# Expert weights on separate semaphores, and down weights issued one expert later

## What is computed

```python
# 16 experts, the best 2 of one group of 4 for each token, width 256
def step(acc, xs):
    wg, wu, wd, cw = xs
    y = (jax.nn.silu(t @ wg) * (t @ wu)) @ wd
    return acc + y.astype(jnp.float32) * cw[:, None], None
acc, _ = lax.scan(step, jnp.zeros(t.shape, jnp.float32), (w_gate, w_up, w_down, comb.T))
```

## Time and profile before

| | us |
|---|---|
| median of 3 runs | 1970.52 |
| lowest and highest | 1969.63, 1974.61 |
| profiled execution, its own time | 1959.03 |
| its span, first to last instruction | 1957.4 |
| experts stage of layer 0, about | 1385 to 1545 |
| experts stage of layer 1, about | 1788 to 1957 |

### The profile page before, as it was taken

One profiled execution on the slowest core, in us unless ns is written; L12 is line 12 of the kernel. 1 busy time (PEld: TensorE's weight loads), 2 busy tenths in 40 slices (PEclk: granted clock), 3 DMA queues, 4 the chain that ended last, 5 costly groups with the idle time before them and its releaser, 6 DMA issues.

```text
span 1957.4 us, 25950 instructions
## 1 busy us (share of the span) xinstructions
PE 1897.8 (97%) x9760; PEld 1005.7 (51%) x9760; DVE 750.1 (38%) x1637; ACT 546.4 (28%) x1187; POOL 732.5 (37%) x1065
## 2 busy tenths in 40 slices
PE   8999999999999999999999999999998899999988
PEld 6644556656457455565665455654443344444433
DVE  1343443433221243434336563843532401334424
ACT  3243432214321334422124222742211221012110
POOL 0767676765666667676700012100110100001101
PEclk9999999999999999999999999999999999999999
DMA  7332343244344353333384312042799722047996
GB/s 292 123 109 101 127 148 121 87 144 142 137 169 141 105 199 107 135 138 116 138 335 162 129 38 86 2 181 98 284 366 369 252 91 86 30 186 256 362 377 247
DMA packets 71706, 328.70 MB, mean 168 GB/s; under 512 B 8680, under 2 KB 11174, under 8 KB 56998
## 3 DMA queue, kind: packets, MB, share of 16 engines
q1 hardware_dynamic: 41688, 217.00, 29.9%
q0 software_dynamic: 26736, 98.58, 14.5%
q10 hardware_dynamic: 3168, 11.54, 1.5%
HBM read 288.29 MB, written 38.80 MB: 167 GB/s over the span
## 4 chain that ended last, share of the span: by engine, by line
PE 88%; DMA 5%; DVE 3%; issue 2%; ACT 1%; DVEq 1%; SPq 0%; POOL 0%; ACTq 0%; POOLq 0%
PE psA L464 26%; PE psA L1815 10%; PE psA L456 9%; PE psA L1950 6%; PE psA L1852 6%; PE psA L627 6%; PE psSO L1968 4%; PE psT L443 3%; DMA pool_mem<-in_w_dn 3%; PE psA L505 3%; PE psSO L534 3%; PE psSO L544 2%; DVE pool_mem L2894 1%; PE psSO L565 1%; PE psSO L600 1%
## 5 line engine op out<-in xcount | busy, mean ns | idle before, releaser
L464 PE MATMUL psA<-gB,pool_mem 128*128 128x512 f32 x1024 | 455.3, 597 | 0.0
L395 POOL TENSOR_TENSOR pool_mem<-pool_mem,cs 128x256 f32<-128x256 f32 x448 | 269.3, 634 | 126.4 <-DMA pool_mem<-in_mod_w 125.8
L464 PEld LDWEIGHTS psA<-gB,pool_mem 128*128 128x128 f32 x1024 | 189.5, 190 | 224.2 <-issue 224.2
L399 POOL TENSOR_TENSOR pool_mem<-pool_mem 128x256 f32<-128x256 f32 x336 | 248.1, 766 | 30.9 <-issue 22.9
L1815 PE MATMUL psA<-pool_mem 128*128 128x512 f32 (+1 forms) x528 | 210.7, 558 | 6.0 <-DVE pool_mem L1584 3.4
L456 PE MATMUL psA<-pool_mem,gB 128*128 128x256 f32 (+2 forms) x768 | 190.8, 404 | 1.7 <-ACT gB L797 1.2
L1764 POOL DMA_INDIRECT pool_mem<-xs_scratch,idx x38 | 35.4, 932 | 391.0 <-DVE idx L2568 361.1
L456 PEld LDWEIGHTS psA<-pool_mem,gB 128*128 128x128 f32 x768 | 144.6, 191 | 44.3 <-issue 8.3
L1950 PE MATMUL psA<-pool_mem 128*32 128x512 f32 (+1 forms) x896 | 146.2, 618 | 10.9 <-DMA pool_mem<-in_w_dn 10.9
L1815 PEld LDWEIGHTS psA<-pool_mem 128*128 128x128 f32 x528 | 100.3, 192 | 109.8 <-issue 99.8
L1852 PE MATMUL psA<-pool_mem 128*128 128x512 f32 x256 | 113.9, 595 | 0.8 <-issue 0.8
(11 more groups left out here) (345 smaller groups left out, 2371.0 us busy)
## 6 DMA issues: line engine op xcount, KB each, us to landing
pool_mem<-in_w_gu SPq DMA_DIRECT2D x32, 2048.0 KB, 13.8
pool_mem<-in_mod_w POOLq DMA_DIRECT2D x56, 1024.0 KB, 7.8
pool_mem<-in_w_dn SPq DMA_DIRECT2D x32, 1024.0 KB, 12.6
pool_mem<-in_w_qk SPq DMA_DIRECT2D x24, 1024.0 KB, 5.1
ys_scratch<-pool_mem POOLq DMA_DIRECT2D x1, 11264.0 KB, 42.1
ys_scratch<-pool_mem ACTq DMA_DIRECT2D x22, 512.0 KB, 11.5
pool_mem<-in_odd_w_in SPq DMA_DIRECT2D x5, 2048.0 KB, 9.7
pool_mem<-in_w_out SPq DMA_DIRECT2D x4, 2048.0 KB, 8.1
```

The source lines that it names most:

```text
L395: nc.gpsimd.tensor_tensor(wm[:, b, k], wm[:, b, k], c_all[:, k].to_broadcast([P, MCH]), ALU.mult)
L399: nc.gpsimd.tensor_tensor(wm[:, b, k], wm[:, b, k], wm[:, b, n + k], ALU.add)
L464: m = nc.tensor.matmul(psA[:, n % 2, :], w(i), src[:, k, :], start=(i == 0), stop=(i == len(ks) - 1))
```

## The change

It gives gate and up weights the semaphores `gate_up_loaded` (five) and down weights `down_loaded` (three, by u modulo 3). The gate and up product waits for gate and up weights alone. The down product gets waits for its own down weights. Since there are three semaphores for up to five transfers, dn(u) is issued only when dn(u - 3) has landed. And in SyncE's list dn(u) moves behind gu(u + 1), for u = 4 to 14.

```diff
-LOADED = [32 * len(USES[b::EXP_BUFS]) for b in range(EXP_BUFS)]
+LOADED = [16 * len(USES[b::EXP_BUFS]) for b in range(EXP_BUFS)]
+DOWN_SEMS = 3
+DOWN_LOADED = [16 * len(USES[b::DOWN_SEMS]) for b in range(DOWN_SEMS)]
...
-                sp.dma_start(gu_w[b], rows(d["w_gu"][l][e])).then_inc(exp_loaded[b], 16)
+                sp.dma_start(gu_w[b], rows(d["w_gu"][l][e])).then_inc(gate_up_loaded[b], 16)
...
-                sp.dma_start(down_w[b], rows(d["w_dn"][l][e])).then_inc(exp_loaded[b], 16)
+                if l or u >= DOWN_SEMS:
+                    sp.wait_ge(down_loaded[u % DOWN_SEMS], DOWN_LOADED[u % DOWN_SEMS] * l + 16 * (u // DOWN_SEMS))
+                sp.dma_start(down_w[b], rows(d["w_dn"][l][e])).then_inc(down_loaded[u % DOWN_SEMS], 16)
...
+                behind = None
                 for u in range(EARLY + 1, EXPERTS):
                     e = expert_of(u)
                     load_gate_up(l, u, e)
-                    load_down(l, u, e)
+                    if behind:
+                        load_down(l, *behind)
+                    behind = (u, e)
+                load_down(l, *behind)
...
-                        pe.wait_ge(exp_loaded[u % EXP_BUFS], LOADED[u % EXP_BUFS] * l + 32 * (u // EXP_BUFS + 1))
+                        pe.wait_ge(gate_up_loaded[u % EXP_BUFS], LOADED[u % EXP_BUFS] * l + 16 * (u // EXP_BUFS + 1))
+
+                def down_weights(c):
+                    for r, _, _, _ in PARTS[c]:
+                        u = USES.index(r)
+                        pe.wait_ge(down_loaded[u % DOWN_SEMS], DOWN_LOADED[u % DOWN_SEMS] * l + 16 * (u // DOWN_SEMS + 1))
...
                 def down(c):
                     b = c % 2
+                    down_weights(c)
                     pe.wait_ge(ht_copied, RUNS * l + c + 1)
```

More of the change, by code:

```diff
@@ L1481, in per_layer @@
         return [sem(f"{name}{l}") for l in range(DEPTH)]
-    exp_loaded = [sem(f"exp_loaded{b}") for b in range(EXP_BUFS)]
+    gate_up_loaded = [sem(f"gate_up_loaded{b}") for b in range(EXP_BUFS)]
+    down_loaded = [sem(f"down_loaded{b}") for b in range(DOWN_SEMS)]
     idx_moved = sem("idx_moved")
@@ L1929, in gate_up_first @@
                         pe.wait_ge(gb_copied, (6, 8)[l])
-                        pe.wait_ge(exp_loaded[0], LOADED[0] * l + 32)
+                        pe.wait_ge(gate_up_loaded[0], LOADED[0] * l + 16)
                     for k in ks:
```

## The result

| | median of timed runs, us | range | profiled execution | span |
|---|---|---|---|---|
| before | 1970.52 (3 runs) | 1969.63 to 1974.61 | 1959.03 | 1957.4 |
| changed | 1943.35 (3 runs) | 1940.44 to 1943.80 | 1940.44 | 1938.9 |

The ratio is 0.9853, 95% interval 0.9827 to 0.9879: 27.2 us less between the medians, and 29.0 (23.8 to 34.1) by the ratio. The profiled executions differ by 18.6 us only, and the forecast was 20.5. The direction and the mechanism came out as forecast; the size, between the medians, was 6.7 us larger.

The account below looks back on a forecast made before the run. TensorE, busy nearly all the span, was taken to bound the kernel, so only its waits and slowed instructions could be won. 22.5 less 1.0 remaining and 1.0 added waits gave 20.5 us off the median: 1950.0 us, range 1943 to 1961.

Parts of the forecast that it names:

- The four waits and the slow clock behind them: TensorE's weight waits in both experts stages and the matmuls slowed after them: removing all saves at most 22.5 us.
- Run 9: Each layer's first weight wait, ahead of a gate and up product, 5.18 and 5.77 us: expected to vanish.
- Run 11, the count of bytes: Ahead of the last gate product: 41.0 MB in layer 0 at 370 GB/s, gu(15) landing at 1508.4 and 1913.6 us.
- Remaining waits: Weight waits left ahead of the last gate products: 1.0 us in all, bounds 0 and 1.9.
- Added waits on TensorE: 19 new waits per layer at the down products: 1.0 us in all, bounds nothing and 3.4 us.
- Added waits on SyncE: In SyncE's load queue, dn(u) waiting for dn(u - 3) to land: no cost.
- dn(14) and dn(15) at the end: Last down loads, now ending the load chain: landing at about 1514 us, 8 us before their down product needs them.
- The sum: Whole kernel: 22.5 - 1.0 - 1.0 = 20.5 us saved, subtracted from the median to give 1950.0 us.
- A: Rival, chance 0.20: rate stays 356 GB/s, waits of 3.2 and 4.4 us remain before the last gate products; 1958.3 us.
- B: Rival, chance 0.09: DMA engines bound the experts stages at 345 GB/s or less; gain only 5 us, 1965.5 us.
- C: Rival, chance 0.05: always-queued weight loads slow the gathers, so transposes wait in every run; slower, 1970 to 1990 us.
- D: Rival, chance 0.06: unprofiled runs hold longer weight waits, so more than 24 us is won; 1944 us.

Follow-up runs that it names:

- experiment 13: Kernel before, old order and semaphores, without five down-weight transfers (dn(8), dn(9), dn(10), dn(14), dn(15)) in both layers: median 1943.33 us, ratio 0.9896.
- experiment 3: Changed kernel with the loads back in the old order, so only the semaphores are split: median 1955.56 us, ratio 0.9931 to the kernel before.
- experiment 4: Kernel before with the new load order alone, one semaphore still covering both transfers of an expert: median 1962.63 us, ratio 0.9975.
- experiment 2: Changed kernel timed and traced again without any edit: median 1942.44 us, ratio 0.9873 to the kernel before.
- experiment 8: Changed kernel timed and traced a third time without any edit: median 1944.18 us, ratio 0.9883 to the kernel before.
- experiment 6: Changed kernel with every added wait at the down products written three times: median 1944.22 us, ratio 0.9885 to the kernel before.
- experiment 9: Kernel before with dn(4) issued behind gu(5) instead of ahead of it: median 1965.30 us, ratio 0.9995.
- experiment 10: Changed kernel with dn(4) put back directly behind gu(4): median 1942.14 us, ratio 0.9887 to the kernel before.

## Why the prediction was right in kind and short in size

**The four waits and the slow clock behind them (22.5 us).** Right. Against the 60.1 us of experiment 13, which has no such waits, the five traces of before give 22.1 to 24.0 us, mean 23.2; the profiled execution on which I summed gave 22.7. This term was short by 0.7.

**Run 9.** Right: no wait in either layer. Experiments 3 and 4 show that it takes both parts, the semaphore (own dn no longer counted) and the order.

**Run 11, the count of bytes.** Right in its result, by two errors that nearly cancel, which is luck. I took 370 GB/s for a queue that is never empty, and 380 was measured; I put 41.0 MB ahead of gu(15)'s landing, and 380 GB/s x 112.1 us = 42.6 MB came. It landed at 1507.7, 2.0 us ahead of a stage clock that itself ran 2.0 us early, so 1509.7 against my 1508.4. In layer 1 it landed at 1878.8 + 21.4 = 1900.2; that stage's first hidden transposes come 12.1 us earlier than before (1785.7), so 1912.3 against my 1913.6. Remaining waits: 0.3 us in this trace, 1.4 in experiment 2 and 1.6 in experiment 8, and by the table the changed kernel's stretches are 1.2 us above those with no waits, against 1.0 forecast.

**Added waits on TensorE (1.0 us).** Wrong in size. Experiment 6 puts them at nothing that can be measured, in timed runs and in a stretch of 92.7 us. My upper bound took the 0.09 us between two kinds of runs for the price of a wait.

**Added waits on SyncE, and dn(14) and dn(15) at the end.** Right: no matmul of a down product waited for weights (the weight loads ahead of them, which overlap other matmuls, show 3.0 us in five places), and gu(15) went out 21 us and dn(14) 9 us earlier than before. dn(14) and dn(15) had landed by 1513.2, against my 1514, and the down product of run 11 started at 1520.5.

**The sum.** The mechanism held; the step that failed is the size of the sum's terms. "Waits added on TensorE" was put at 1.0 us and measured nothing, and the ceiling, put at 22.5 from one execution, measured 23.2 as the mean of five. 23.2 less 1.2 of remaining waits is 22.0 us, where the sum had 22.5 - 1.0 - 1.0 = 20.5. That is 1.5 of the 6.7 us by which the result exceeded the forecast. The other 5.2 have no term in the sum, which was subtracted from a median 11.5 us above the execution that it was read from.

By the ratio, three sets of timed runs give 29.0 (23.8 to 34.1), 25.0 (21.0 to 29.1) and 23.0 us (18.5 to 27.3); by the medians 27.2, 23.8 and 21.6. The last two hold 22.0; the first, with three runs on each side, begins at 23.8. So part of the 5.2 is the draw of the first runs: before had a median of 1970.5 there and 1964.2 to 1966.3 in the four later sessions, while the changed kernel stayed at 1942.4 to 1944.2. The rest of it stays open. The traces put at most about 3.3 us outside the stretches, most of it around the start of layer 1's stage, where two of five traces of before lose 5.8 and 4.0 us and one of three of the changed kernel 2.4. Layer 0's start varies too: the profiled execution of before loses 2.7 us there. Whether the new order makes such losses rarer is not shown: experiments 9 and 10 don't isolate it in dn(4), and experiment 13 keeps the old order and has only one trace.

**The profile's own time.** I noted that the profiled execution lay 11.5 us below the median and did not ask why. About 6 of it is the late copy of ScalarE at the end, missing in that one execution. Since the changed kernel's trace has it, the profiled executions differ by only 18.6 us. That my 20.5 lies near 18.6 is partly luck: without that one absent stall they would differ by about 24.5.

**Rivals.** A asked for 3.2 and 4.4 us ahead of run 11 and 356 GB/s; neither came. B needed 345 GB/s or less. C: transposes wait for gathered rows only at a stage's start, as before (5.3 us in three places against 4.0 in two). D put a surplus on weight waits that are longer in slower executions; its size was nearer than the forecast's (1944 against 1943.4 measured), but its reason does not agree with the table above. The rule of the Trainium skill on HBM bandwidth ("DMA: Bandwidth & Descriptors", Specifications, about 358 GB/s for a core) is not a cap here: 380 GB/s stood for 112 us, and that includes 512 KB stores to HBM.

## What to carry to other kernels

When two inputs are needed at different times, give each its own semaphore and issue them in the order in which they are needed. Do both at once: in the traces the parts alone took 10 and 2 us off the stretches with the waits, together 22. In a fixed issue list look for a load that stands behind a wait it does not need; gu(15) went out 21 us earlier by one swap. And before subtracting from a median, ask what distinguishes the profiled execution from it: one stall present or absent at the end was worth 5.9 us, nearly the whole 6.7 by which the sum missed. Read a sum of this kind from several traces.

## What the runs showed of the hardware

- The 16 DMA engines moved 380 GB/s over 112 us of mixed loads (16 and 8 KB per partition), gathers and stores, and 424 (changed) and 435 (before) in the 10 us from 1490. A DMA share of 1.00 does not mean that no more goes through: the plateau of before had 1.00 at 365 GB/s, the same stretch of the changed kernel 1.01 at 379.
- Idle times of 5.2 to 6.1 us ahead of run 9's product cost 2.1 to 3.0 us more in it in the five traces of before, 6.1 and 6.7 us in experiment 9 1.7 and 1.4, and 8.1 and 8.3 us in experiment 4 2.7 and 2.3; so in these traces the cost does not grow with the idle time. The granted clock was 0.67 in the window of the earlier trace rows, which is between its two levels. Kept busy during the wait, TensorE took 7.07. Idle times of 2.2 to 2.7 us ahead of run 11 cost either 0 or 1.7 us, from one execution to the next.
- 76 more waits on TensorE (38 more instructions), on conditions already met and behind queued matmuls, cost nothing measurable: 0.9885 against 0.9883, and 92.7 us in both for the stretch up to run 8.
- One copy by ScalarE at the end comes about 4 us late in every trace but one; the same copy in layer 0 does not (0.69 us ahead of the product behind it, in each trace). In its program it stands behind a branch over a long part that is not executed; what it waits for there the trace does not name, and I have not tested it.
